# Hybrid layers of a two-block model: attention output turned in another chunk order, two blocks of it inside the last projection; the differential heads' rstd by root and reciprocal

## The reference, cut to what matters

```
h = rms_norm_2(x, pre_w)
proj = h @ w_in
a_q, a_k, a_v, a_g, b_q, b_k, b_v, b_g, c_q, c_kv, c_kr, c_g = split(proj)
y_a = diff_attention(...)             # 4 heads: a = p1 - lam * p2; o = a @ v
                                      # o = rms_norm_2(o, subln_w, 1e-5) * (1 - lam_init)
y_b = sliding_window_attention(...)   # 16 heads, with sinks
y_c = causal_attention(...)           # 4 heads
y = concat([y_a, y_b, y_c]) * silu(concat([a_g, b_g, c_g]))
out = y @ w_out
return x + rms_norm_2(out, post_w)
```

## Time and profile before

| what | value |
|---|---|
| median of 3 runs | 2828.7 us |
| profiled execution | 2829.58 us, span 2827.4 us |
| PE busy | 2682.7 us, 95% |
| DVE busy | 1899.8 us, 67% |
| ACT busy | 1273.1 us, 45% |
| chain that ended last | PE 81%, DVE 10%, ACT 5% |
| DMA queue q1 (weights) | 408.99 MB, 45.3% of 16 engines |
| last steps and output projection of hybrid layer 0 | from 2237 us of the span |
| the same of hybrid layer 1 | from 2690 us of the span |

### The profile page before, as it was taken

One profiled execution on the slowest core, in us unless ns is written; L12 is line 12 of the kernel. 1 busy time (PEld: TensorE's weight loads), 2 busy tenths in 40 slices (PEclk: granted clock), 3 DMA queues, 4 the chain that ended last, 5 costly groups with the idle time before them and its releaser, 6 DMA issues.

```text
span 2827.4 us, 36465 instructions
## 1 busy us (share of the span) xinstructions
PE 2682.7 (95%) x13605; PEld 2209.7 (78%) x13605; DVE 1899.8 (67%) x2677; ACT 1273.1 (45%) x2016; POOL 0.2 (0%) x4
## 2 busy tenths in 40 slices
PE   5998899999999989999999999988999989999988
PEld 2576678888778878888888888777878777878867
DVE  5755567877888567767767767856656555656654
ACT  6653222122322644534444445546455645544553
POOL 0000000000000000000000000000000000000000
PEclk9999999999999999999999999999999999999989
DMA  8763456655465433333333333454644455544453
GB/s 310 267 217 128 132 152 191 206 162 178 171 217 199 146 90 91 101 111 93 101 103 102 93 102 102 141 186 150 190 140 151 147 208 177 170 149 149 150 178 134
DMA packets 406588, 437.16 MB, mean 155 GB/s; under 512 B 22718, under 2 KB 286536, under 8 KB 404936
## 3 DMA queue, kind: packets, MB, share of 16 engines
q1 hardware_dynamic: 397760, 408.99, 45.3%
q10 hardware_dynamic: 8712, 26.59, 2.6%
HBM read 427.14 MB, written 8.39 MB: 154 GB/s over the span
## 4 chain that ended last, share of the span: by engine, by line
PE 81%; DVE 10%; ACT 5%; issue 2%; DMA 1%; ACTq 0%; DVEq 0%; SPq 0%
PE ps L1118 14%; PE ps L1119 14%; PE ps L1120 14%; PE ps L1121 9%; PE ps L1123 9%; PE ps L1122 9%; DVE wl L1779 3%; DVE acc L1850 2%; ACT wh L577 1%; PE ps L1428 1%; PE ps L1142 1%; PE ps L1449 1%; PE ps L1144 1%; PE ps L1433 1%; PE ps L1720 1%
## 5 line engine op out<-in xcount | busy, mean ns | idle before, releaser
L1779 DVE TENSOR_TENSOR wl<-raw,wh 128x1024 fp32r<-128x1024 f32 (+2 forms) x784 | 822.0, 1079 | 477.5 <-ACT wh L577 466.2
L577 ACT ACTIVATE wh<-raw 128x1024 fp32r<-128x1024 f32 (+2 forms) x784 | 714.3, 943 | 853.3 <-PE ps L1120 493.7
L1118 PE MATMUL ps<-hTh,wh 128*128 128x512 f32 (+1 forms) x2124 | 783.7, 369 | 38.1 <-DVE wl L1779 28.4
L1119 PE MATMUL ps<-hTl,wh 128*128 128x512 f32 (+1 forms) x2124 | 772.0, 363 | 0.0
L1120 PE MATMUL ps<-hTh,wl 128*128 128x512 f32 (+1 forms) x2124 | 770.1, 363 | 0.0
L1121 PE MATMUL ps<-wh,hTh 128*128 128x512 f32 (+1 forms) x1440 | 577.5, 401 | 26.9 <-DVE wl L1779 18.5
L1123 PE MATMUL ps<-wh,hTl 128*128 128x512 f32 (+1 forms) x1440 | 559.9, 389 | 0.0
L1122 PE MATMUL ps<-wl,hTh 128*128 128x512 f32 (+1 forms) x1440 | 559.5, 389 | 0.0
L1118 PEld LDWEIGHTS ps<-hTh,wh 128*128 128x128 f32 x2124 | 405.4, 191 | 110.3 <-DVE wl L1779 29.6
L1119 PEld LDWEIGHTS ps<-hTl,wh 128*128 128x128 f32 x2124 | 405.1, 191 | 62.4 <-issue 0.5
L1120 PEld LDWEIGHTS ps<-hTh,wl 128*128 128x128 f32 x2124 | 404.5, 190 | 63.0
(11 more groups left out here) (295 smaller groups left out, 2029.3 us busy)
## 6 DMA issues: line engine op xcount, KB each, us to landing
raw<-in_ada_w_dram SPq DMA_DIRECT2D x96, 1024.0 KB, 5.2
raw<-in_w_in_dram SPq DMA_DIRECT2D x88, 1024.0 KB, 5.1
raw<-in_od_w_in_dram SPq DMA_DIRECT2D x256, 320.0 KB, 3.5
raw<-in_ev_w_in_dram SPq DMA_DIRECT2D x192, 256.0 KB, 3.9
raw<-in_w_out_dram SPq DMA_DIRECT2D x32, 1024.0 KB, 5.1
raw<-in_ev_w_out_dram SPq DMA_DIRECT2D x16, 1024.0 KB, 5.2
raw<-in_od_w_out_dram SPq DMA_DIRECT2D x16, 1024.0 KB, 5.1
x_save<-arena ACTq DMA_DIRECT2D x6, 1024.0 KB, 5.4
```

The source lines that it names most:

```text
L577: nc.scalar.activation(wh[:, ch.spl, part], raw[:, ch.raw, part], ACT.Copy).then_inc(s_hi, 1)
L1118: nc.tensor.matmul(out, w_h, x_h, start=first, stop=False, skip_group_check=True)
L1119: nc.tensor.matmul(out, w_h, x_l, start=False, stop=False, skip_group_check=True)
L1779: nc.vector.tensor_tensor(wl[:, ch.spl, part], raw[:, ch.raw, part], wh[:, ch.spl, part].bitcast(F32), ALU.subtract).then_inc(s_lo, 1)
```

## The change

1. `move ag` goes from half 96 to half 98, so on ACT and DVE it comes behind the score of pair 13 and ahead of that pair's normalising for the flip (and `move` names its block by the table, since half 98 belongs to another).
2. The rstd of a differential head is made by one Sqrt on ACT and a reciprocal on DVE, in place of Ln and Exp on ACT.
3. The turned blocks come in the order of columns b, b, a, c (`Y_ORDER`), and the chunks of w_out for block n = 0 are loaded and multiplied in that order. Turn 0 comes after half 101 into bank 7, turn 1 after half 102 (and behind `weigh 13`) into bank 6. The other six are made ahead of the second, third, fifth, sixth, eighth and ninth tile of the projection. Turn 0 waits for pair 9, turn 1 for the last flip, turn 2 (bank 4) for pair 13, turn 6 for `move cg`.
4. ACT and DVE split chunk 0 of w_out and write out turn 0 already behind half 101; `move cg` comes between turns 3 and 4; chunk 2 is split between turns 5 and 6, so ahead of the DMA issues; DVE waits for the post-norm weight only where it first needs it.

```diff
-for _h, _name in (..., (88, "av"), (96, "ag")):
+for _h, _name in (..., (88, "av"), (98, "ag")):
...
+Y_ORDER = (1, 2, 0, 3)
+Y_PAIR = [2 * c + h for c in Y_ORDER for h in range(2)]
+Y_BANK = (7, 6, 4, 5)
+Y_AT = {1: 2, 2: 3, 4: 4, 5: 5, 7: 6, 8: 7}
...   ACT, rstd
-                        step(nc.scalar.activation(ors, oss, ACT.Ln, scale=1.0 / P, bias=C("eps")[:, 1:2])).done()
-                        nc.scalar.activation(ors, ors, ACT.Exp, scale=-0.5).then_inc(s_os, 1)
+                        nc.scalar.activation(ors, oss, ACT.Sqrt, scale=1.0 / P, bias=C("eps")[:, 1:2]).then_inc(s_os, 1)
...   DVE, rstd
                         dve.wait_ge(s_os, count(4, h + 1))
+                        step(nc.vector.reciprocal(ors, ors)).done()
...   PE
+                def turn_y(n):
+                    g = Y_PAIR[n]
+                    if n == 0:
+                        pe.wait_ge(s_45, count(len(USE45), USE45.index("weigh 9") + 1))
+                        pe.wait_ge(s_67, count(len(USE67), USE67.index("turn ak") + 1))
+                    elif n == 1:
+                        pe.wait_ge(s_67, count(len(USE67), len(USE67)))
+                    elif n == 2:
+                        pe.wait_ge(s_45, count(len(USE45), len(USE45)))
+                    elif n == 6:
+                        moved("cg")
+                    if n >= 4:
+                        pe.wait_ge(s_ytl, count(YT, n - 3))
+                    ...
+                def y_ahead(k):
+                    if k in Y_AT:
+                        turn_y(Y_AT[k])
+                    if k % 2 == 0:
+                        pe.wait_ge(s_ytl, count(YT, k // 2 + 1))
...   (in the loop over the halves)
+                    if i == 2 * NPROJ - 3:
+                        turn_y(0)
+                    if i == 2 * NPROJ - 2:
+                        turn_y(1)
...   (behind it)
-                pe.wait_ge(s_45, count(len(USE45), len(USE45)))
-                pe.wait_ge(s_67, count(len(USE67), len(USE67)))
                 moved("ag")
-                for g in range(4):
-                    turn_y(g)
...   ACT
+                    if i == 2 * NPROJ - 3:
+                        hi(st.chunk("hyb", L, NPROJ))
+                        high_turned(0)
+                high_turned(1)
+                hi(st.chunk("hyb", L, NPROJ + 1))
+                high_turned(2)
+                high_turned(3)
+                after(2 * NPROJ - 1)
+                high_turned(4)
+                high_turned(5)
+                hi(st.chunk("hyb", L, NPROJ + 2))
+                high_turned(6)
+                high_turned(7)
...   DVE: the same order with lo and low_turned, and
-                dve.wait_ge(s_gl, L * 16 + 16)
-                for m in range(2, 18):
+                for m in range(3, 18):
...
                     if m % 4 == 1 and m < 16:
                         n = m // 4 - 1
+                        if n == 0:
+                            dve.wait_ge(s_gl, L * 16 + 16)
```

More of the change, by code:

```diff
@@ L557, in _ @@
                     ch = st.chunk("hyb", L, NPROJ + i)
-                    load(ch, [(slot4(ch), one(layer(w_out2[:, i % 4], L)[:, :, :, (i // 4) * BLK:(i // 4 + 1) * BLK]))])
+                    load(ch, [(slot4(ch), one(layer(w_out2[:, Y_ORDER[i] if i < 4 else i % 4], L)[:, :, :, (i // 4) * BLK:(i // 4 + 1) * BLK]))])
             for u in range(4):
@@ L985, in move @@
                 def move(name, i):
-                    b, _ = done(i)
+                    done(i)
+                    b = BNUM[name]
                     if name in ("cq", "ckv"):
@@ L1075, in after, with high_turned @@
                             {"score": score, "flip": flip, "weigh": weigh}[verb](int(arg))
+                def high_turned(n):
+                    g = Y_PAIR[n]
+                    act.wait_ge(s_yt, count(YT, n + 1))
+                    act.wait_ge(s_used, st.chunk("hyb", L, NPROJ - 4 + Y_ORDER[n // 2]).piece(1))
+                    nc.scalar.activation(hTh[:, 2 * g:2 * g + 2, 0:SEQ], ps[:, Y_BANK[n % 4], :].rearrange("p (a b) -> p a b", a=2),
+                                         ACT.Copy).then_inc(s_yth, 1)
                 hyb_split(L, 4, (0,))
-                for i in range(6, 2 * NPROJ):
+                for i in range(6, 2 * NPROJ - 1):
                     if i + 3 < 2 * NPROJ:
@@ L1096, in hyb_layer @@
                     load_x(u, x_rows, XBN)
-                for m in range(2, 16):
+                for m in range(3, 16):
                     hi(st.chunk("hyb", L, NPROJ + m))
@@ L1273, in gate_rows, with out_block @@
                 nc.tensor.matmul(ps[:, 6 + r % 2, :], ones, gate_block(r), start=True, stop=True).then_inc(s_gb, 1)
-            def out_block(chunks, T, bank, before=None, after=None):
+            def out_block(chunks, T, bank, before=None, after=None, order=range(4)):
                 for c, ch in enumerate(chunks):
@@ L1280, in out_block @@
                             pe.wait_ge(s_lo, ch.half(t // 2))
-                        k = 4 * c + t
+                        k = 4 * order[c] + t
                         if before:
-                            before(k)
+                            before(4 * c + t)
                         for m in range(T):
@@ L1762, in hyb_layer @@
                         free_banks(L * 3 + 6, n)
-                    out_block([st.chunk("hyb", L, NPROJ + 4 * n + c) for c in range(2 if n == 3 else 4)], 2, 2 * (n % 2), y_ahead if n == 0 else None)
+                    out_block([st.chunk("hyb", L, NPROJ + 4 * n + c) for c in range(2 if n == 3 else 4)], 2, 2 * (n % 2), y_ahead if n == 0 else None, order=range(4) if n else Y_ORDER)
                 last_chunks([st.chunk("hyb", L, NPROJ + 14), st.chunk("hyb", L, NPROJ + 15)], 1 if L == 0 else None)
@@ L2600, in hyb_layer @@
                     after(i)
[L2602 to L2609 removed]
+                    if i == 2 * NPROJ - 3:
+                        lo(st.chunk("hyb", L, NPROJ))
+                        low_turned(0)
+                low_turned(1)
                 lo(st.chunk("hyb", L, NPROJ + 1))
[L2611 to L2612 removed]
+                low_turned(2)
+                low_turned(3)
                 after(2 * NPROJ - 1)
[L2614 to L2617 removed]
+                low_turned(4)
+                low_turned(5)
+                lo(st.chunk("hyb", L, NPROJ + 2))
+                low_turned(6)
+                low_turned(7)
+                for m in range(3, 18):
                     if m < 16:
```

39 lines of the change are left out of this document (13 added, 26 removed).

## The result

The changed kernel takes 2803.4 us (median of 4 runs, 2801.7 to 2804.6), the kernel before 2828.4 in the same comparison (2827.1 to 2832.4): ratio 0.9909, 95% interval 0.9892 to 0.9926, 25 us less. The forecast was 2801, in a range of 2795 to 2811. The profiled execution has a span of 2801.9 us against 2827.4.

What follows compares the result with a forecast made beforehand. PE, busy 95% of the span, was taken to bound the kernel, with time lost in its waits and slow matmuls. Gains 12.5 + 16.4 + 1.0 + 0.1 + 0.5 = 30.5, less 2.2, gave 28.3 us: 2801 us, range 2795 to 2811.

Steps and rivals of the forecast that it cites:

- The likeliest case: Whole kernel: the forecast itself, 2801 us within 2796 to 2807, chance 0.79.
- What it said would show it: Changed profile: one wait of about 2.5 us ahead of the last flip, none ahead of weigh 12, turn 2 or 6.
- From the flip to the end of block n = 0: PE after pair 13's flip: 34.7 us after the change, gaining 12.5 us in layer 0 and 16.4 in layer 1.
- The four waits: PE around the start of layer 0's output projection: 3.2, 3.0, 2.5 and 1.3 us, 10.0 in sum, would go.
- the walk: Step-by-step times from the flip over PE, ACT and DVE: 1.8 us spare at turn 2, 0.1 us wait at chunk 3.
- the first rival, late chunks: Block n = 0: chunks 2 and 3 come late, 8.6 us less gain than forecast, 2810 us; chance 0.15.
- From the score to the flip: Pair 13: 12.7 us with the moved gate, wait of 2.5 ahead of flip; gain 1.0 in layer 0, 0.1 in layer 1.
- Slow matmuls: Behind the wait ahead of the flip: 5.5 on average at 0.2 us each, 1.1 us per layer, 2.2 lost in sum.
- The bound: Slow matmuls behind the flip's wait: loss between 0 and 2.8 us per layer, 0 to 5.6 in both.
- The rstd: Differential heads: root comes 1.5 us earlier in pairs 10 to 12, 2.8 in pair 13; earlier bank reads gain 0.5 us.
- The rule on table sets: Skill page: exp and ln share a table set, sqrt another; its 2.7 us switch would make the sum 27.8.
- The rival on the other side: Last halves and block n = 0: lower clock stays, 26.4 us more per layer, 2852 us; chance 0.03.

Runs made afterwards that it cites:

- e9: Kernel before with only the new order of turns, chunks and late post-norm wait; Ln and Exp kept, gate at half 96: 2803.3 us, ratio 0.9914.
- e4: Changed kernel with the gate (move ag) back at half 96, all else as changed: 2798.7 us, ratio 0.9891 to the kernel before.
- e5: Changed kernel with Ln and Exp again for the rstd, gate at half 98: 2807.0 us, ratio 0.9931 to the kernel before.
- e2: Changed kernel with the gate (move ag) at half 99 instead of 98: 2793.9 us, ratio 0.9881 to the kernel before.
- e11: Repeat of e2 beside other kernels, gate at half 99 in the changed kernel: 2793.9 us, ratio 0.9880 to the kernel before.
- e6: Kernel before with the root and reciprocal alone, old order, gate at half 96: 2825.5 us, ratio 0.9990.
- e3: Changed kernel with the gate (move ag) at half 97 instead of 98: 2800.8 us, ratio 0.9906 to the kernel before.
- e7: Kernel before with one edit, DVE waits for the post-norm weight only where it first uses it: 2826.6 us, ratio 0.9999.
- e8: Kernel before with the edit of e7, and ACT rounds chunk 2 ahead of its DMA issues: 2819.6 us, ratio 0.9974.
- e1: The changed kernel run again unaltered, as base on the same chip: 2802.0 us, ratio 0.9906 to the kernel before.

## Why the prediction was right

The likeliest case came about, by its own steps, with 25.0 us for 28.3. What it said would show it did: no wait ahead of `weigh 12`, one ahead of the last flip, the last root without a load and 0.30 us long, no wait at turns 2 and 6. What it did not foresee is how the parts share the gain: the order alone gives nearly all of it (e9), and the moved gate takes away about what the root brings (e4, e5).

**From the flip to the end of block n = 0.** Predicted 34.7 us and some for slow matmuls; measured 36.35 and 37.6. The four waits went, as the walk said. Its times, measured from the flip and less the 1.6 us of slow matmuls in layer 0: turn 0 at 3.1 (3.0 predicted), root of pair 13 done 8.1 (7.9), DVE's reading done 9.7 (9.6), turn 2 at 11.5 (11.4), `move cg` done 19.9 (19.5), turn 6 at 21.6 (21.4), first half of chunk 2 split at 22.2 (22.0), ACT at chunk 3 26.8 (26.9). The margins of 1.8 us at turn 2 and of next to nothing at chunk 3 (0.2 us measured) held, so the first rival, late chunks, did not happen.

**From the score to the flip.** Predicted 12.7, measured 12.92 in both layers; the wait 2.5, measured 2.9. The stretch without a wait was set at 10.2 and is 9.9 (e2, e11). The term was a little kind: I set the moved gate at 1.0 and 0.1 us of gain against the kernel before. Measured against the kernel that keeps it at 96 but has all else (e4), it is a loss of 0.85 us per layer, without the slow matmuls. The root had already shortened the old wait from 1.9 to 1.2 (e6), which I had put down to the gate.

**Slow matmuls.** The term that was mis-sized. I took 5.5 per layer at 0.2 us, 2.2 us in all; there were 8 and 12, which by the last column against e4 cost 1.6 and 2.8 us, 4.4 in all. The bound (up to 2.8 per layer) held. This and the two 0.2 us above are 2.6 of the 3.3 us that the forecast was off. The average left out two spells of the kernel before, 7 and 11 slow matmuls behind the waits of 3.25 and 2.11 us for the first turned block; with them it is 6.7 per layer, 2.7 us in all. Where within the bound the number would fall was chance: behind a wait as long, e3 had none in layer 0.

**The rstd.** Predicted: no load for pair 13, 2.8 us earlier "where it counts". The load was gone, but it hardly counted: without the root PE waits 0.68 us ahead of turn 2 (e9), not 2.5. The order, with turn 2 behind the first tile, covers most of it. The 0.5 us for the earlier reads of the weighed banks was counted in layer 0 alone; it is 0.6 in each layer, from the score of pair 10 to that of pair 13. In all the root is worth 3.0 us at equal clock in the changed order (e5); the medians say 3.6 to 5.

**The rule on table sets.** Ln and Exp were loaded one after the other in e5 and e9 as in the earlier trace rows. From the rstd of pair 10 to `move cg` each layer has eleven table loads before and seven after. The Trainium skill, "ScalarE: Activation LUTs", section on table sets, has ln and exp in one set, with one load for the pair; the traces show two, so that set was not used here, and the measurement decides. By the page's price of a switch the prediction's sum would have been 0.5 us less.

**The rival on the other side** (the lower clock stays to the end of the block) did not come about in any profile: no slow spell in these stretches had more than 13 slow matmuls, and in the new order the transposes between matmuls did not bring one on.

## What to carry to other kernels

Four waits in a row on the busiest engine were not four lacks of speed: another order took them away (e9). What is ready is turned first, what is late last, and the transposes stand between products instead of in front of them. When a step is moved away from one wait on an in-order engine, read what is queued behind its new place, here the normalising for the next flip: against its old place the gate cost 3 to 5 us at 98 and gave 5 at 99. And where a profile names one releaser for a wait, ask what came second; the edit that removes only the first is worth the gap between the two (e7), the edit that removes both is worth the wait (e8).

## What the runs showed of the hardware that was not expected

After waits of the same length PE fell to the lower clock or did not: after 3.08 us in e3 with 12 slow matmuls in layer 1 and none in layer 0; after 2.9 us with 8 and 12 in the changed kernel, 7 and 12 in e1 and 8 and 8 in e5; after 1.9 us with 9 and 8 in e9 and with 8 and none in the kernel before; after 1.21 and 0.56 not at all in both layers of e4 and e6. The spells had 5 to 9 or 11 to 13 slow matmuls, whatever the wait. With no wait over 0.35 us (e2, e11) there were none in these stretches. So a wait can be dearer than it looks: in the changed kernel 0.85 us more than in e4 from score to flip came with 1.6 and 2.8 us of slow matmuls behind it.

A slow spell costs nothing where PE would have waited anyway. Behind the same wait of 2.5 us the sixteen transposes take 1.97 us in layer 0 of the kernel before and 3.10 in layer 1, and the wait behind them is 3.25 and 2.11 us: the next turned block is ready 5.2 us after their start in both.

A table load of 1.28 us was followed at once by the next activation (2244.79 + 1.28, sigmoid at 2246.09 in the changed kernel): no further cost of the load is seen there.
